# Projections of a two-layer trunk in transposed layout: weights stationary, no transposes of projected tiles

## The reference

```python
def retention_mixer(h, w_in, w_out):            # layer 1: 8 heads, dk 256, dv 512, chunks of 128 tokens
    q, k, v, gate = split(h @ w_in)             # 2048 + 2048 + 4096 + 4096 columns
    scores = (qc @ kc.T) * decay                # within a chunk; a state carries over chunks
    o = scores @ vc + (qc @ state) * q_decay
    o = (o - mean(o)) * rsqrt(var(o) + EPS)     # per head
    return (silu(gate) * o) @ w_out

def nsa_mixer(h, w_in, ...):                    # layer 2: 16 heads in 4 groups, dh 128
    q, kc, vc, ks, vs, kw, vw, g, z = split(h @ w_in)   # 2048, 6 x 512, 48, 2048 columns
    k_cmp, v_cmp = block MLPs over kc, vc (blocks of 32 tokens, stride 16)
    # three softmax branches with ALiBi: compressed, selected blocks, window;
    # with 256 tokens all blocks are selected and the window covers all
    o = gate0 * o_cmp + gate1 * o_slc + gate2 * o_win
    return (silu(z) * o) @ w_out
```

## Time and profile before

| | |
|---|---|
| median of 3 runs | 1273.14 us |
| the profiled execution, span from first to last instruction | 1273.0 us |
| TensorE busy | 1249.7 us, 98% |
| TensorE weight loads busy (beside matmuls) | 1018.4 us, 80% |
| VectorE busy | 682.9 us, 54% |
| ScalarE busy | 540.3 us, 42% |
| mean granted TensorE clock | 0.996 |
| transfers | 221.61 MB, 174 GB/s |

### The profile page before, as it was taken

The page is one execution under the profiler, slowest core; times in us unless marked ns, Lnnn a source line. Parts: engine busy times, 40 slices in busy tenths (PEclk is TensorE's granted clock), DMA queues, the critical chain, the costliest instruction groups (busy, mean ns, idle before and its releaser), DMA issues.

```text
span 1273.0 us, 14955 instructions
## 1 busy us (share of the span) xinstructions
PE 1249.7 (98%) x5710; PEld 1018.4 (80%) x5710; DVE 682.9 (54%) x744; ACT 540.3 (42%) x672; POOL 59.3 (5%) x53
## 2 busy tenths in 40 slices
PE   7999999999999999999999999999999999999997
PEld 6878788788788788788888888888878687887875
DVE  5545365364373463464464576444446475665765
ACT  6344243342342343343334355233346374472553
POOL 1010100100100100100100111000000000000000
PEclk9999999999999999999999999999999899999999
DMA  9636645546456465564564485646434234444432
GB/s 334 238 132 199 198 165 176 187 165 206 157 187 207 142 208 179 165 209 154 165 231 143 161 272 198 201 132 231 166 107 158 99 133 165 163 134 137 160 104 96
DMA packets 129302, 221.61 MB, mean 174 GB/s; under 512 B 6768, under 2 KB 39744, under 8 KB 129008
## 3 DMA queue, kind: packets, MB, share of 16 engines
q1 hardware_dynamic: 127360, 213.94, 50.4%
q0 software_dynamic: 1712, 7.07, 1.8%
q10 hardware_dynamic: 192, 0.08, 0.0%
HBM read 218.96 MB, written 2.10 MB: 174 GB/s over the span
## 4 chain that ended last, share of the span: by engine, by line
PE 98%; DVE 1%; DMA 0%; ACT 0%; issue 0%; POOL 0%; POOLq 0%; DVEq 0%; ACTq 0%
PE acc L924 28%; PE acc L926 28%; PE acc L925 28%; PE side L961 2%; PE side L1058 2%; PE side L1143 2%; PE side L1084 1%; PE side L925 1%; PE side L926 1%; PE side L924 1%; PE side L1130 1%; PE side L1145 1%; PE side L953 1%; PE side L997 1%; PE side L1006 1%; PE side L1004 1%
## 5 line engine op out<-in xcount | busy, mean ns | idle before, releaser
L629 DVE TENSOR_TENSOR w_lo<-w_raw,w_hi 128x2048 fp32r<-128x2048 f32 x199 | 452.2, 2287 | 282.9 <-ACT w_hi L409 280.8
L924 PE MATMUL acc<-w_hi,hT_hi 128*128 128x512 f32 x1280 | 509.8, 398 | 3.4 <-DVE vw L662 1.5
L926 PE MATMUL acc<-w_hi,hT_lo 128*128 128x512 f32 x1280 | 499.9, 391 | 0.0
L925 PE MATMUL acc<-w_lo,hT_hi 128*128 128x512 f32 x1280 | 499.4, 390 | 0.0
L409 ACT CAST w_hi<-w_raw 128x2048 fp32r<-128x2048 f32 x199 | 374.3, 1908 | 130.2 <-PE acc L926 129.3
L924 PEld LDWEIGHTS acc<-w_hi,hT_hi 128*128 128x128 f32 x1280 | 241.2, 188 | 55.7 <-issue 5.4
L925 PEld LDWEIGHTS acc<-w_lo,hT_hi 128*128 128x128 f32 x1280 | 241.3, 189 | 50.6 <-issue 1.9
L926 PEld LDWEIGHTS acc<-w_hi,hT_lo 128*128 128x128 f32 x1280 | 240.9, 188 | 51.1
L924 PE MATMUL acc<-w_hi,yT_hi 128*128 128x512 f32 x264 | 104.3, 395 | 0.0
L926 PE MATMUL acc<-w_hi,yT_lo 128*128 128x512 f32 x264 | 102.9, 390 | 0.0
L925 PE MATMUL acc<-w_lo,yT_hi 128*128 128x512 f32 x264 | 102.8, 389 | 0.0
(11 more groups left out here) (145 smaller groups left out, 767.9 us busy)
## 6 DMA issues: line engine op xcount, KB each, us to landing
w_raw<-in_ret_w_in SPq DMA_DIRECT2D x192, 512.0 KB, 4.6
w_raw<-in_nsa_w_in SPq DMA_DIRECT2D x112, 512.0 KB, 4.6
w_raw<-in_ret_w_out SPq DMA_DIRECT2D x64, 512.0 KB, 4.8
w_raw<-in_nsa_w_out SPq DMA_DIRECT2D x32, 512.0 KB, 4.9
res<-in_x SPq DMA_DIRECT2D x4, 512.0 KB, 8.9
arena<-in_nsa_cmp_w_k POOLq DMA_DIRECT2D x1, 2048.0 KB, 12.8
arena<-in_nsa_cmp_w_v POOLq DMA_DIRECT2D x1, 2048.0 KB, 12.2
out<-w_raw SPq DMA_DIRECT2D x4, 512.0 KB, 3.3
```

The source lines that it names most:

```text
L629: dve.tensor_tensor(w_lo[:, s, :, :], w_raw[:, s, :, :], w_hi[:, s, :, :].bitcast(F32), ALU.subtract).then_inc(lo_done, 1)
L924: pe.matmul(o, xT_hi[:, k0 + i, tok], w_hi[:, s, i, :], start=a, stop=False)
L925: pe.matmul(o, xT_hi[:, k0 + i, tok], w_lo[:, s, i, :], start=False, stop=False)
L926: ins = pe.matmul(o, xT_lo[:, k0 + i, tok], w_hi[:, s, i, :], start=False, stop=z)
```

## The change

The projections of q, k of retention, and of kc, vc, ks, kw, q and z of layer 2, use a new function `chunk_T`. In it 128 features by 128 weight columns are stationary and the 256 tokens of `hT` move, so that the result has columns on partitions and tokens along a row. A chunk is 4 feature blocks x 4 column tiles x 3 = 48 matmuls. `hT_hi` and `hT_lo` become two halves of one tensor `hT`. `transpose_q`, `transpose_z` and the sets for q, k and for the raw tiles go, with the copies behind them. The token factor, now along the row, is either applied by a multiply with a row that holds the factors on all partitions (`take_T`), or, in retention, left off q and k: the factor of the key's token is applied with the decay mask, and that of the query's token cancels in the head's normalization, where eps is multiplied by the mean square instead. The retention scores move from behind chunk 5 to behind chunk 4. z is taken by VectorE and then put through SiLU in place by ScalarE.

```diff
+        hT = sb("hT", [P, KT, 2, S], F32R)
+        rstd_row = stage[:, 0, 0:S]
...
+            def chunk_T(q, c, pair, uses, between=None):
+                s = c % RING
+                if s == 0 and not known(uses, 0):
+                    pe.wait_ge(acc_free[pair], uses)
+                n = 4 * q + s
+                by_halves = known(n, 0)
+                pe.wait_ge(*((first_lo, 1) if by_halves else (lo_done, n + 1)))
+                for i in range(KPC):
+                    k = KPC * s + i
+                    if i == KPC // 2 and between:
+                        between()
+                    if by_halves and i == KPC // 2:
+                        pe.wait_ge(lo_done, 1)
+                    for m in range(4):
+                        o = acc[pair][m // 2][:, (m % 2) * S:(m % 2 + 1) * S]
+                        w = slice(m * P, (m + 1) * P)
+                        pe.matmul(o, w_hi[:, s, i, w], hT[:, k, 0, :], start=(k == 0 and m % 2 == 0), stop=False)
+                        pe.matmul(o, w_hi[:, s, i, w], hT[:, k, 1, :], start=False, stop=False)
+                        ins = pe.matmul(o, w_lo[:, s, i, w], hT[:, k, 0, :], start=False, stop=(k == KT - 1 and m % 2 == 1))
+                ins.then_inc(chunk_done, 1)
...
@@ TensorE, retention
-                    in_chunk(q + c // 4, c, (0, 1, 0)[c // 4], (u0, u1, u0 + 1)[c // 4])
+                    (chunk_T if c < 4 else in_chunk)(q + c // 4, c, (0, 1, 0)[c // 4], (u0, u1, u0 + 1)[c // 4])
...
                     if c == 4:
+                        pe.wait_ge(qT_ready, h + 1)
                         pe.wait_ge(acc_free[0], u0 + 1)
-                        if not first:
-                            pe.wait_ge(side_read, side_reads(h))
-                        transpose_tiles(stage, (0, 1)).then_inc(qkT_psum, 1)
-                    if c == 5:
-                        pe.wait_ge(qT_ready, h + 1)
-                        pe.wait_ge(kT_ready, h + 1)
...
@@ TensorE, layer 2
-                in_chunk(KV_Q + i, c, ...)
+                (in_chunk if i in (3, 6) else chunk_T)(KV_Q + i, c, ...)
...
+                if c == 2:
+                    pe.wait_ge(rstd_done, 2)
+                    pe.wait_ge(hT_done, 2 * CG - 1)
+                    for t in range(TT):
+                        ins = pe.matmul(side[0][:, t * P:(t + 1) * P], rstd[:, 1, t:t + 1].to_broadcast([P, P]), ident[:, :], start=True, stop=True)
+                    ins.then_inc(rstd_row_psum, 1)
...
@@ VectorE
+            def take_T(chunk, pair, to, scale=1.0):
+                dve.wait_ge(chunk_done, chunk)
+                for i in range(2):
+                    row = bass.AP(rstd_row.tensor, rstd_row.offset, [rstd_row.ap[0], [0, 2], [1, S]])
+                    ins = dve.scalar_tensor_tensor(out=to[:, 2 * i:2 * i + 2, :], in0=acc[pair][i][:, :].rearrange("p (a b) -> p a b", a=2),
+                                                   scalar=scale, in1=row, op0=ALU.mult, op1=ALU.mult)
+                ins.then_inc(acc_free[pair], 1)
...
+                    if c == 3:
+                        take_T(4 * q + 4, 1, silu_zT)
                     if c == 7 and "q" in kinds:
-                        take(4 * q + 8, 0, stage, 1)
+                        take_T(4 * q + 8, 0, qhT, float(DH) ** -0.5)
...
@@ ScalarE
-                    if c == 3:
-                        take_z(q)
+                    if c == 4:
+                        silu_z(g)
...
-                    if c == at["zT"]:
-                        take_zT(g)
-                    if c == at["qT"] and "q" in kinds:
-                        take_q(g + 1)
```

More of the change, by code:

```diff
@@ L223, in trunk, with kv_taken, q_taken, z_taken @@
         KV_GROUPS = len(KV_COLS)
+        def kv_taken(i):
+            pair = (i + 1) % 2
+            return acc_free[pair], KV_USES[pair] + i // 2 + 1
+        def q_taken(g):
+            return (acc_free[0], nsa_uses(g)[0] + 1)
+        def z_taken(g):
+            return (acc_free[1], nsa_uses(g)[1] + 1)
         def nsa_q(g):
@@ L249, in nsa_uses @@
             return tuple(u if first else u + 3 * g - 2 for u in NSA_USES)
-        SLOTS = {12: dict(scores=(1, 3, 5), factors=(2, 4, 6), probsT=(1, 3, 5, 7), zT=6, values=8, qT=9, next=10, next_factors=11),
-                 8: dict(scores=(0, 2, 4), factors=(1, 3, 5), probsT=(0, 2, 4, 6), zT=5, values=7, qT=7, next=7, next_factors=8)}
+        SLOTS = {12: dict(scores=(1, 3, 5), factors=(2, 4, 6), probsT=(1, 3, 5, 7), values=8, next=10, next_factors=11),
+                 8: dict(scores=(0, 2, 4), factors=(1, 3, 5), probsT=(0, 2, 4, 6), values=7, next=7, next_factors=8)}
         FIRST_SCORES = 4 * KV_GROUPS - 3
@@ L465, in retention @@
                         squares(0, 2 + c)
-                    if c == 4:
-                        act.wait_ge(qkT_psum, h + 1)
-                        act.copy(qT, side[0][:, :].rearrange("p (a b) -> p a b", a=2)).then_inc(qT_ready, 1)
+                    if c == 3:
+                        act.wait_ge(chunk_done, n0 + 4)
+                        act.copy(qT, acc[0][0][:, :].rearrange("p (a b) -> p a b", a=2)).then_inc(qT_ready, 1)
                     if c == 7:
                         act.wait_ge(chunk_done, n0 + 8)
+                        if first:
+                            act.wait_ge(rstd_done, 1)
                         for t in range(TT):
@@ L499, in _ @@
                 squares(1, j)
[L501 to L505, removed]
             def compress(n):
@@ L525, in _ @@
                     norm_high(1, 3)
[L526 to L536, removed]
+                if c == 3:
+                    act.wait_ge(rstd_row_psum, 1)
+                    act.wait_ge(squares_done, 2 * CG)
+                    act.copy(rstd_row, side[0][:, 0:S]).then_inc(rstd_row_ready, 1)
                 if c in (5, 9):
@@ L562, in take_pT, with silu_z @@
                 ins.then_inc(pT_ready, 1)
[L564 to L574, removed]
+            def silu_z(g):
+                act.wait_ge(*z_taken(g))
+                act.activation(silu_zT, silu_zT, ACT.Silu).then_inc(zT_ready, 1)
             def high_y(g):
@@ L749, in make_window @@
             def make_window(n):
[L751 removed]
+                dve.wait_ge(*kv_taken(n))
                 if n == 0:
@@ L803, in _ @@
                 if c in (3, 7, 11, 19, 23):
-                    take(n, (c // 4 + 1) % 2, stage, 1)
+                    if c == 3:
+                        dve.wait_ge(rstd_row_ready, 1)
+                    if c == 7:
+                        dve.wait_ge(window_ready, 1)
+                    if c == 19:
+                        dve.wait_ge(hid_psum, 2)
+                    to = {3: rawT, 7: rawT, 11: ksT[:, :, NC:NC + S], 19: qhT, 23: kwT}[c]
+                    take_T(n, (c // 4 + 1) % 2, to, float(DH) ** -0.5 if c == 19 else 1.0)
                 if c in (4, 8):
@@ L1003, in retention @@
                         pe.wait_ge(acc_free[1], u1 + 1)
+                        if not first:
+                            pe.wait_ge(side_read, side_reads(h))
                         pe.matmul(side[0][:, :], sT[:, 0:P], v_sb[:, 0, :], start=True, stop=True)
@@ L1161, in sparse @@
                     if kind == "z":
-                        in_chunk(q, c, 1, u1)
+                        chunk_T(q, c, 1, u1)
                     elif kind == "q":
-                        in_chunk(q + 1, c, 0, u0, step)
+                        chunk_T(q + 1, c, 0, u0, step)
                     else:
@@ L1174, in sparse @@
                         head_scores(g, at["scores"].index(c) + 1)
-                    if c == at["zT"]:
-                        transpose_z(g, sum(x <= c for x in at["probsT"]))
-                    if c == at["qT"] and not last:
-                        transpose_q(g + 1, (acc_free[0], u0 + 1))
                     if c == at["next"] and not last:
```

61 lines of the change are left out of this document (18 added, 43 removed).

## The result

The changed kernel takes 1277.07 us (median of 9 runs, 1276.34 to 1278.01), the kernel before 1273.62 us (9 runs, 1271.37 to 1274.92) beside it. The ratio is 1.0029, 95% interval 1.0020 to 1.0039: slower by 3.5 us, where 1265.5 and "faster" were forecast. The time is that of rival B, 1277.0.

The account below looks back on a forecast made before the run. TensorE was taken as the bound, time being a sum over what it issues: 1273.0 + 14.1 - 18.0 + 0.55 - 4.3 = 1265.3, stated as 1265.5 us, range 1250 to 1279.

Parts of the forecast that it names:

- rival B: Every narrow step collides with its weight load: 0.120 us a step, +25.6 us, time 1277.0; chance 0.18.
- Part 1: Transposed chunks: 1920 wide matmuls become 3840 narrow ones at 0.117 us, the gate matmuls' step; +14.1 us.
- The lower bound: Narrow matmuls of the transposed chunks at half a wide step, 0.1133 us, adding 0.0 us.
- The upper bound: Narrow matmuls of the transposed chunks at 0.120 us, the first single gate step shown, adding 25.6 us.
- Rival A: The narrow step is free, locking at 0.1133 us, half a wide one; time 1251.4, chance 0.20.
- The rule of the Trainium skill: A matmul costs its columns at full clock plus about 2.5 ns; narrow matmuls then add +5.2 us, whole 1256.6.
- Parts 2 to 5: Transposes dropped, -18.0 us; token-factor row, +0.55; stall at end of group 0, -4.3; other engines, nothing.
- The transposes: Transposes of projected tiles go: 20 sets of 8 on TensorE at 0.90 us each, -18.0 us.
- The row of factors: Two fp32 matmuls behind the third chunk of layer 2, +0.55 us, their wait for GpSimd's factors covered.
- Group 0: Stall at its end: next chunk begins 3.6 us earlier and the clock stays up; -4.3 us beyond the transposes.
- rival C: The clock still falls behind group 0: time 1268.9, chance 0.12.
- Rival D: TensorE's instruction supply can't keep up with twice the instructions; at 0.120 us a pair, time 1277.0; chance 0.05.

Follow-up runs that it names:

- e15: Control: changed kernel with longer weight rings, shorter scratch and a later weight copy, split weights of transposed projections shifted 0 columns; 1277.20 us.
- e13: Changed kernel, whole computation, split weights of transposed projections kept 80 columns (320 B) further along their ring slot; 1265.65 us, 0.9949 of the kernel before.
- e3: Changed kernel with the stationary weight slices of narrow steps beginning 48 columns apart instead of 128, so projected values differ; 1266.93 us.
- e4: Changed kernel with wide chunks streaming 384 of 512 weight columns, except matmuls that open a sum; 1157.39 us.
- e2: Changed kernel loading only 64 of 128 stationary weight columns in 14 of 16 feature blocks of the transposed chunks; 1256.17 us.
- e5: Changed kernel with wide chunks loading only 64 of 128 token columns, except matmuls that open or close a sum; 1283.82 us.
- e1: Changed kernel with transposed chunks moving only 128 of 256 token columns for 15 of 16 feature blocks; 1248.76 us.
- e6: Changed kernel with 32 B of unused memory ahead of hT; 1281.99 us.
- e8: Changed kernel with 128 B of unused memory ahead of hT; 1290.97 us.
- e10: Changed kernel with wide chunks streaming 384 columns that begin at a different constant per chunk, first matmul of a chunk whole; 1157.62 us.
- e12: Changed kernel, whole computation, split weights of transposed projections kept 16 columns (64 B) further along their ring slot; 1266.96 us.
- e14: Changed kernel, whole computation, split weights of transposed projections kept 112 columns (448 B) further along their ring slot; 1269.23 us, 0.9971 of the kernel before.

## Why the prediction was wrong

- **Part 1, the failed step.** "I take 0.117, the row of the same form; it comes from weights at other offsets than those of the change, and only 48 in a row." The measured term is +25.2 us instead of +14.1, and that is the whole error: 11 us. The size of this term was wrong; that the time is a sum of TensorE's steps held. The form (128x128 loaded, 256 columns moving) does not fix the price; e15 against e13, and e3, show the same form at 0.1200, 0.1170 and 0.1172 with nothing changed but where the slices begin. The offset was named as a doubt and kept in the range, but the value that went into the sum took it to be without effect. What lies beneath, why these starts cost 13.3 ns and others less, stays open.
- The reason given for a narrow step over half a wide one, that a wide step hides its load fully, isn't borne out: a wide step carries 13.3 ns of surcharge as well (e4: still 13.3 with 384 columns). The lower bound, half a wide step, halved this surcharge too. The upper bound was taken from one single step that read 0.12; it is also the columns plus the whole surcharge, 106.7 + 13.3 = 120.0, and that sum could have been made from the earlier trace rows.
- **Rival B was right in its time and its step** (0.120, from 0.119 on), and its ground, that matmuls aligned as in the change need not have the gates' mean, is what e3 and e13 show. It was given 0.18. Its mechanism, "every narrow step collides with its load", fits e2 (half the load, half the surcharge) but is not shown by it, and as a rule it fails in e5.
- **Rival A** took "settled steps" for "free steps". Nearly all steps did settle, as it said, but at 0.120. A run of 142 at 0.1133 exists (e13), so the price is real; it needs another start.
- **The rule of the Trainium skill** ("TensorE: Matmul & The Clock Gate", section on the back-to-back issue gap: columns and about 2.5 ns) gave an estimated 1256.6, farther off than the forecast. Its form, a fixed amount for each matmul, describes the aligned steps of this kernel; its size doesn't: 13.3 ns here. That form with the amount from the earlier trace rows would have given +25.6 us.
- **Parts 2 to 5 held.** With the step at 0.1170 (e13) the forecast's sum, 1265.5, meets the measured 1265.65, which tests these parts together. That e13's mean is the forecast's 0.117 is luck: it is a mix of 15 chunks at 0.1133 and 65 at 0.1178. The transposes are gone (no matmul from the staging tile is left). The row of factors cost 0.44 for 0.55, without a wait. Group 0: 6.22 - 2.63 = 3.6 us as forecast, the clock stayed at 1.00, so rival C did not come. TensorE has no new wait for another engine.
- **Rival D** is out: 142 pairs in a row at 0.1133 and three chunks at 0.1117 in e1, with the same instructions, leave no room for a supply of instructions at 0.120 a pair.

A set of transposes was worth 0.90 us, while four chunks in narrow form cost 192 x 0.1199 - 96 x 0.2267 = 1.26 us. At 0.1199 each of the 20 projections that were changed loses 0.36 us, and only the stall behind group 0 gives 4.3 back; at 0.1170 the form costs 0.70, and each gains 0.20.

## What to carry to other kernels

When a change splits matmuls, write a step as its columns at the granted clock plus a surcharge, read the surcharge from the rows of the kernel at hand, and count it once for each matmul; don't halve it with the width. A row of the same form prices a step only if the stationary slices and the moving operand also begin alike. If a stream of matmuls bounds the kernel, where operands begin is a thing to try: here an offset of 320 B for the split weights of the narrow steps turned a loss of 3.5 us into a gain of 7.6. Move one operand at a time: the padding of e6 to e8, which moved the input of all steps, made the kernel slower.

## What the runs showed of the hardware

- Between starts of back-to-back fp32r matmuls, each with its own load of 128 columns and aligned as in this kernel: 226.7 ns for 512 columns, 173.3 for 384, 120.0 for 256, each the columns at 2.4 GHz and 13.3 ns. With 128 columns it was 111.7 and not the 66.7 of that sum: another limit, the load or the issue of a pair.
- The values at which steps settled were 113.3, 120.0, 173.3, 226.7 and 233.3 ns, and 117.8 as the mean of a short pattern. The start of either operand moves a step (the stationary one in e13, the moving one in e6 to e8 and e10): 113.3 to 120.0 for 256 columns, 226.7 to 233.3 for 512. One alignment was best for wide steps and worst for narrow ones.
- The same chunk at the same addresses can settle at 113.3 or 117.8 from one pass of a loop to another (e13, second and third head). In e12 to e14 the value never changed between chunks that follow each other directly (117 places), only where other matmuls stood between them.
- The busy mean of a load goes with the start of the slices: 193 ns in the kernel after and 192 to 193 in e15, where steps are 120.0; 189 to 190 in e13 and e3; 188 for the wide chunks. It doesn't measure the step, for in e1 it is 193 with steps of 111.7. That the two reads, of the load and of the stream, meet in SBUF is argued from e2 and the offsets, not shown.
